# Four layer norms of a three-block kernel: two wide operations on VectorE in place of centring on ScalarE, gain on VectorE and bias on GpSimd

## What is computed

```python
def layer_norm(x, g, b):
    xf = x.astype(jnp.float32)
    mu = jnp.mean(xf, axis=-1, keepdims=True)
    var = jnp.mean(jnp.square(xf - mu), axis=-1, keepdims=True)
    return ((xf - mu) * lax.rsqrt(var + LN_EPS) * g + b).astype(x.dtype)
...
        # second block
        x = layernorm_2(DEEPNORM_ALPHA * x + mix, ln1_g[l], ln1_b[l])
        hid = jax.nn.silu(jnp.einsum('bsd,df->bsf', x, w_gate[l])) * jnp.einsum('bsd,df->bsf', x, w_up[l])
        ffn = jnp.einsum('bsf,fd->bsd', hid, w_down[l])
        x = layernorm_2(DEEPNORM_ALPHA * x + ffn, ln2_g[l], ln2_b[l])
...
        # third block
        x = layer_norm(DEEPNORM_ALPHA_3 * x + mix, ln1_g[l], ln1_b[l])
        xa = memory_cross_attention(x, mem, xa_wq[l], xa_wk[l], xa_wv[l], xa_wo[l])
        x = layer_norm(DEEPNORM_ALPHA_3 * x + xa, ln2_g[l], ln2_b[l])
        ff = hierarchical_moe(x, ...)
        x = layer_norm(DEEPNORM_ALPHA_3 * x + ff, ln3_g[l], ln3_b[l])
```

## Time and profile before

| | before |
|---|---|
| median of 3 runs | 3304.01 us (3303.87 to 3304.07) |
| the profiled execution | 3298.76 us |
| its span | 3297.1 us |
| TensorE busy | 3034.3 us, 92% |
| VectorE busy | 1455.9 us, 44% |
| ScalarE busy | 684.7 us, 21% |
| GpSimd busy | 131.8 us, 4% |
| mean granted TensorE clock | 0.953 |

### The profile page before, as it was taken

The page is one execution under the profiler, slowest core; times in us unless marked ns, Lnnn a source line. Parts: engine busy times, 40 slices in busy tenths (PEclk is TensorE's granted clock), DMA queues, the critical chain, the costliest instruction groups (busy, mean ns, idle before and its releaser), DMA issues. The chain is left out here.

```text
span 3297.1 us, 38666 instructions
## 1 busy us (share of the span) xinstructions
PE 3034.3 (92%) x15110; PEld 2168.6 (66%) x15110; DVE 1455.9 (44%) x2574; ACT 684.7 (21%) x1546; POOL 131.8 (4%) x148
## 2 busy tenths in 40 slices
PE   8779998999999889986999999998989986999997
PEld 4367765888868668885688887876766634333332
DVE  1564424324453667367543354424654232333335
ACT  1131112220010543570111001113531211111111
POOL 1000000000000200001000000000000011000000
PEclk9889999999999979997999999997889997999998
DMA  9112211223221102201223222222012107999995
GB/s 359 67 51 77 77 58 71 83 77 109 77 79 59 45 27 77 77 1 39 77 77 98 82 98 81 77 80 77 1 65 76 52 15 296 423 424 423 424 424 221
DMA packets 129894, 420.48 MB, mean 128 GB/s; under 512 B 6705, under 2 KB 35778, under 8 KB 108242
## 3 DMA queue, kind: packets, MB, share of 16 engines
q1 hardware_dynamic: 121842, 379.48, 30.1%
q10 hardware_dynamic: 3024, 23.59, 1.8%
q0 software_dynamic: 4880, 15.35, 1.3%
HBM read 394.81 MB, written 23.59 MB: 127 GB/s over the span
## 5 line engine op out<-in xcount | busy, mean ns | idle before, releaser
L775 PE MATMUL bank<-arena 128*128 128x256 f32 x5152 | 1125.3, 381 | 30.5 <-issue 15.5
L775 PEld LDWEIGHTS bank<-arena 128*128 128x128 f32 x5152 | 984.0, 191 | 172.1 <-issue 22.8
L1070 PE MATMUL bank<-arena 128*128 128x256 f32 x1652 | 358.7, 380 | 6.3 <-PEq L1217 2.7
L1070 PEld LDWEIGHTS bank<-arena 128*128 128x128 f32 x1652 | 314.6, 191 | 50.3 <-issue 7.4
L176 PE MATMUL bank<-arena 128*128 128x512 f32 (+7 forms) x804 | 252.1, 470 | 37.3 <-PEq L3297 11.5
L176 PEld LDWEIGHTS bank<-arena 128*128 128x128 f32 (+3 forms) x804 | 137.1, 195 | 146.7 <-issue 125.3
L423 PE MATMUL bank<-arena 128*128 128x512 f32 x384 | 167.7, 597 | 4.2 <-PEq L1622 2.0
L3737 DVE TENSOR_TENSOR arena<-arena,bank 128x512 f32<-128x512 f32 x128 | 87.7, 687 | 139.1 <-PE bank L3641 136.8
L839 DVE TENSOR_TENSOR arena<-arena 128x1024 f32<-128x1024 f32 x46 | 56.3, 1223 | 182.7 <-PE bank L775 179.3
L423 PEld LDWEIGHTS bank<-arena 128*128 128x128 f32 x384 | 73.1, 191 | 95.5 <-issue 95.5
L3641 PE MATMUL bank<-arena 128*128 128x512 f32 x256 | 123.2, 616 | 4.4 <-DVE arena L3723 4.4
(11 more groups left out here) (540 smaller groups left out, 3572.0 us busy)
## 6 DMA issues: line engine op xcount, KB each, us to landing
arena<-in_moe_w_gate_dram SPq DMA_DIRECT2D x64, 1024.0 KB, 16.4
arena<-in_moe_w_up_dram SPq DMA_DIRECT2D x64, 1024.0 KB, 18.5
arena<-in_moe_w_down_dram SPq DMA_DIRECT2D x32, 2048.0 KB, 23.9
arena<-in_w_in_dram SPq DMA_DIRECT2D x29, 2048.0 KB, 7.9
arena<-in_w_ff_dram SPq DMA_DIRECT2D x16, 2048.0 KB, 7.7
x_slots<-arena ACTq DMA_DIRECT2D x8, 2048.0 KB, 33.1
arena<-in_w_out_dram SPq DMA_DIRECT2D x8, 2048.0 KB, 7.7
arena<-in_w_gate_dram SPq DMA_DIRECT2D x11, 1024.0 KB, 5.4
```

What stands on the lines that cost most here:

```text
L775: last = pe.matmul(bank[:, m, :], lhsT, rhs, start=fresh and m == 0 and k == 0, stop=k == 3, skip_group_check=True)
L1070: last = pe.matmul(bank[:, m, :], x[:, k, m * P:(m + 1) * P], w[:, k, :], start=opening and m == 0 and k == 0, stop=k == w.shape[1] - 1, s ...
```

## The change

For every tile, VectorE now does `(x - mean) * gain` in one operation while ScalarE takes the root, then inverts the root, then does `x * inverse + bias` in a second one. ScalarE's centring, VectorE's shift and gain operations, GpSimd's bias additions and VectorE's extra bias addition for the last tile go, and with them their semaphores. VectorE's copy of tile i-2 now stands behind the tile's second wide operation, where it stood before the reciprocal. The diff of `down_and_layer_norm`; `sevens_and_layer_norm` is changed in the same way:

```diff
@@ down_and_layer_norm
         def ready(i):
-            return (normed, normed.at(i + 1)) if i < NT - 1 else (last_normed, last_normed.at(1))
+            return normed, normed.at(i + 1)
...
                 dve.tensor_scalar(sd[:, i:i + 1], mv[:, i, 1:2], 1.0, eps, ALU.mult, ALU.add).then_inc(var.sem,
                                                                                                        var.up())
+                if i == 0:
+                    dve.wait_ge(got.sem, got.at(32))
+                dve.scalar_tensor_tensor(out=x[:, i, :], in0=x[:, i, :], scalar=mv[:, i, 0:1], in1=gain, op0=ALU.subtract,
+                                         op1=ALU.mult).then_inc(gained.sem, gained.up())
+                dve.wait_ge(root.sem, root.at(i + 1))
+                dve.reciprocal(sd[:, i:i + 1], sd[:, i:i + 1]).then_inc(order.sem, order.up())
+                dve.wait_ge(order.sem, order.sent)
+                dve.wait_ge(gained.sem, gained.at(i + 1))
+                dve.scalar_tensor_tensor(out=x[:, i, :], in0=x[:, i, :], scalar=sd[:, i:i + 1], in1=bias, op0=ALU.mult,
+                                         op1=ALU.add).then_inc(normed.sem, normed.up())
                 if i >= 2:
                     empty_turned(dve, i - 2, 0).then_inc(emptied_v.sem, emptied_v.up())
-                dve.wait_ge(root.sem, root.at(i + 1))
-                dve.reciprocal(sd[:, i:i + 1], sd[:, i:i + 1]).then_inc(order.sem, order.up())
-                dve.wait_ge(order.sem, order.sent)
-                dve.scalar_tensor_tensor(out=shift[:, i:i + 1], in0=mv[:, i, 0:1], scalar=-1.0, in1=sd[:, i:i + 1],
-                                         op0=ALU.mult, op1=ALU.mult).then_inc(scaled.sem, scaled.up())
-                if i == 0:
-                    dve.wait_ge(got.sem, got.at(32))
-                dve.wait_ge(centred.sem, centred.at(i + 1))
-                dve.tensor_tensor(x[:, i, :], x[:, i, :], gain, ALU.mult).then_inc(gained.sem, gained.up())
-                if i == NT - 1:
-                    dve.wait_ge(gained.sem, gained.at(NT))
-                    dve.tensor_tensor(x[:, i, :], x[:, i, :], bias, ALU.add).then_inc(last_normed.sem, last_normed.up())
...
-            pool.wait_ge(got.sem, got.at(32))
-            for i in range(NT - 1):
-                pool.wait_ge(gained.sem, gained.at(i + 1))
-                pool.tensor_tensor(x[:, i, :], x[:, i, :], bias, ALU.add).then_inc(normed.sem, normed.up())
+        if meanwhile:
+            block.gpsimd(meanwhile)
...
                 act.activation(sd[:, i:i + 1], sd[:, i:i + 1], ACT.Sqrt).then_inc(root.sem, root.up())
-                act.wait_ge(scaled.sem, scaled.at(i + 1))
-                act.activation(x[:, i, :], x[:, i, :], ACT.Identity, bias=shift[:, i:i + 1],
-                               scale=sd[:, i:i + 1]).then_inc(centred.sem, centred.up())
```

More of the change, by code:

```diff
@@ L474, in down_and_layer_norm @@
     x, xT = c.x, c.xT
-    stats, mv, sd, shift = layer_norm_numbers(c)
+    stats, mv, sd, _ = layer_norm_numbers(c)
     gain, bias = rows[:, 0, :], rows[:, 1, :]
[L477 to L480, removed]
+    filled, got, var, root, gained, normed, turned, emptied = (c.sig(n) for n in (
+        "bank_filled", "rows_loaded_scalar", "variance_ready", "root_ready", "gain_applied", "normed", "rows_turned",
+        "bank_emptied_by_scalar"))
+    order, emptied_v = c.sig("vector_order"), c.sig("bank_emptied_by_vector")
     early = len(keys) - tail
@@ L1208, in sevens_and_layer_norm @@
     x, xT = c.x, c.xT
-    stats, mv, sd, shift = layer_norm_numbers(c)
+    stats, mv, sd, _ = layer_norm_numbers(c)
     gain, bias = rows[:, 0, :], rows[:, 1, :]
[L1211 to L1215, removed]
+    filled, got, var, root, gained, normed, turned, emptied = (c.sig(n) for n in (
+        "bank_filled", "rows_loaded_scalar", "variance_ready", "root_ready", "gain_applied", "normed", "rows_turned",
+        "bank_emptied_by_scalar"))
+    order, emptied_v, used = (c.sig(n) for n in ("vector_order", "bank_emptied_by_vector", "tile_added"))
     sevens = RowSevens(c, name, hidden, (1, 0), (5, 0), ((5, 3072), (5, 3584), (9, 2048), (9, 2560)), made)
@@ L1267, in _ @@
                                                                                                        var.up())
-                if i >= 2:
-                    empty_turned(dve, i - 2, 0).then_inc(emptied_v.sem, emptied_v.up())
+                if i == 0:
+                    dve.wait_ge(got.sem, got.at(32))
+                dve.scalar_tensor_tensor(out=x[:, i, :], in0=x[:, i, :], scalar=mv[:, i, 0:1], in1=gain, op0=ALU.subtract,
+                                         op1=ALU.mult).then_inc(gained.sem, gained.up())
                 dve.wait_ge(root.sem, root.at(i + 1))
@@ L1272, in _ @@
                 dve.wait_ge(order.sem, order.sent)
-                dve.scalar_tensor_tensor(out=shift[:, i:i + 1], in0=mv[:, i, 0:1], scalar=-1.0, in1=sd[:, i:i + 1],
-                                         op0=ALU.mult, op1=ALU.mult).then_inc(scaled.sem, scaled.up())
-                if i == 0:
-                    dve.wait_ge(got.sem, got.at(32))
-                dve.wait_ge(centred.sem, centred.at(i + 1))
-                dve.tensor_tensor(x[:, i, :], x[:, i, :], gain, ALU.mult).then_inc(gained.sem, gained.up())
-                if i == NT - 1:
-                    dve.wait_ge(gained.sem, gained.at(NT))
-                    dve.tensor_tensor(x[:, i, :], x[:, i, :], bias, ALU.add).then_inc(last_normed.sem, last_normed.up())
+                dve.wait_ge(gained.sem, gained.at(i + 1))
+                dve.scalar_tensor_tensor(out=x[:, i, :], in0=x[:, i, :], scalar=sd[:, i:i + 1], in1=bias, op0=ALU.mult,
+                                         op1=ALU.add).then_inc(normed.sem, normed.up())
+                if i >= 2:
+                    empty_turned(dve, i - 2, 0).then_inc(emptied_v.sem, emptied_v.up())
             for i in (NT - 2, NT - 1):
@@ L1284, in _ @@
             follow.dve(dve, ((emptied_v, NT), (emptied, NT)))
-        @block.gpsimd
-        def _(pool):
-            pool.wait_ge(got.sem, got.at(32))
-            for i in range(NT - 1):
-                pool.wait_ge(gained.sem, gained.at(i + 1))
-                pool.tensor_tensor(x[:, i, :], x[:, i, :], bias, ALU.add).then_inc(normed.sem, normed.up())
         @block.scalar
```

8 lines of the change are left out of this document (2 added, 6 removed).

## The result

The changed kernel takes 3311.84 us, the median of 14 runs (3300.39 to 3313.87); the kernel before, run beside it, took 3304.73 (14 runs, 3303.75 to 3306.56). The ratio is 1.0018, 95% interval [1.001, 1.0026]: slower by a small amount that can be told from nothing, and outside the forecast range of 3299.0 to 3307.5. The first profiled execution of the changed kernel took 3304.61 us (span 3302.8, clock 0.95), 7.2 us under its own median. That is the first thing to notice: this trace is not one of the usual executions.

The account below looks back on a forecast made before the run. PE was taken to bound the kernel, through its waits and its clock. Terms +2.25 (A), -0.56 (B), +0.30 (C), -2.7 (D) sum to -0.7 us; 3304.01 - 0.7 = 3303.3 us, range 3299.0 to 3307.5.

Parts of the forecast that it names:

- What bounds the kernel: TensorE (PE), busy 92% of the 3297.1 us span: time changes only where PE waits or where its clock does.
- What the change does to a tile: Each tile's norm takes 2.65 us from TENSOR_SCALAR to next operation; VectorE's copy, 0.68 us, becomes late at A, B and C.
- A: Second block's attention output layer norm: wait longer by 0.56 us, clock falls in sixteen matmuls (+1.69); +2.25 us in all.
- B: Second block's down projection layer norm: VectorE saves time per tile, PE starts earlier, gap shrinks to 4.28; -0.56 us.
- C: Layer norm of the third block's mixers' output: PE starts 0.55 us later at an already halved clock; +0.30 us taken.
- the third rival: At A to C PE goes by something earlier than VectorE's copy, so the change wins at all four places: 3300.3, chance 0.04.
- The second rival: Faster: the clock holds at A, 0.56 in place of 2.25, 3301.6; if also at D, 3298.8. Chance 0.20.
- D: Third block's cross attention layer norm, no follower: PE's turns start 2.08 us earlier and the clock recovers somewhat; -2.7 us.
- The constant of 5.25 us: Distance between the kernel before's profiled execution (3298.76 us) and the median of its runs (3304.01), treated as constant.
- The sum of -0.7 us: Total forecast change over the four layer norms: +2.25 - 0.56 + 0.30 - 2.7, with no further clock step.
- the first rival: Slower: PE's later start after A costs further clock steps between A and D, 1.69 each: 3305.0 or 3306.7; chance 0.30.
- The slower rival: The same as the first rival: one more clock step between A and D gives 3305.0, two 3306.7; chance 0.30.

Follow-up runs that it names:

- after_look_1: The changed kernel, without an edit, profiled again: median 3311.26 us over 8 runs, ratio 1.0016; its profiled execution took 3312.04 us.
- after_again: The changed kernel again, without an edit, beside the kernel before: 3312.07 us over 8 runs, ratio 1.0027; its profiled execution took 3300.49 us.
- one_more_copy_at_a: The kernel before, with ScalarE's copy of tile 1 at A made twice and nothing of the change: 3313.64 us, ratio 1.0033.

## Why the prediction was wrong, point by point

**What bounds the kernel: right.** Removing 20 us from ScalarE and 31 us from GpSimd moved nothing of its own. All that PE's shift shows is where PE waited and its clock.

**What the change does to a tile: right.** 2.65 us from TENSOR_SCALAR to the copy, wide operations of 1.27 to 1.29. VectorE's copy is last at A, B and C; the third rival fell.

**A: right, to 0.1 us.** Wait 4.25 (forecast 4.29), sixteen matmuls 5.41 (5.38), together +2.2 against +2.25. The price of the clock, taken from B, was the right one of the three named. The second rival, a clock that holds at A, did not happen in any of the four traces of the changed kernel.

**B: right** (-0.6 against -0.56). **C: right** (wait 5.33 against 5.35; the shift +0.1 and +0.4 against +0.30). **D: right in sum** (-2.8 and -3.0 against -2.7). The wait is 3.85, not 3.4, since PE gets through the turns of the tile before it 0.4 us earlier (before, these waited 0.22 us for GpSimd's bias), and the router's sixteen matmuls take 8.80 and 8.60 us in place of 9.54, so that the clock gave 0.7 to 0.9 back.

**The constant of 5.25 us: right for the kernel before.** It lies in the first 240 us. For the changed kernel the same subtraction would mislead: its three other profiled executions stand 0.8 above, 1.0 above and 11.6 below their medians, since an execution meets the step at 2357 us or doesn't; the one 11.6 below also had the low start, PE's shift -3.9 at 1600 us.

**The sum of -0.7 us is where it failed: terms that were put at nothing.** The step is the first rival, "one more such step costs what it cost at B, 1.69". That mechanism was named rightly: a PE that stands otherwise against the clock loses at further waits, in code that nothing touched; what failed is its price and that the forecast itself put it at nothing. One such step, at 1907 us, cost the +1.7 of that price; with it the sum is +1.0, and the first profiled execution of the changed kernel ends by its shift at +0.9 (from +0.3 to +1.2 in the table). The second, in the sparse attention, was mis-sized: 20.5 us of half clock instead of 3.4, +9.6 up to 2390 us, of which 2.3 come back up to 2435 us, where later low stretches are shorter: +7.3 in place of 1.69. The row that should have warned stands in the page: clock digits of 7, 8 and 8 in the three slices from 2226 to 2473 us, stretches of low clock far longer than behind B. The rival's own row warned too: 28 us at a mean of 0.63 are 28 x 0.37 = 10.4 us of missing clock, and it was priced at 1.69. I priced a step by the shortest one in the trace, where the longest ones set the upper end of the range. The sum of `after_look_1` is +0.7 at 1600 us, then +2.2 + 1.7 - 0.6 + 8.4 + 1.2 - 2.3 + 0.1 - 3.0 = +7.7, in all +8.4 by the steps listed and 8.5 by the shift; its time is 3312.04 - 3303.99 = 8.05 above.

**Rivals and chances.** The slower rival was the true one and had 0.30, the largest of the rivals; but its end was 3306.7. With the second step at its measured size it would have been about 3303.3 + 1.7 + 7.3 = 3312.3; that is hindsight, since no row of the trace before gives the 7.3. What the rows give is that a long step costs up to some 10 us, and a range with one such step would have held the time.

**What stays open.** Why the clock falls for 20.5 us behind a wait of 0.72 us in one execution and holds in another is not settled. By the place against the clock's last return the two differ by 0.02 us, and that sorts the traces at hand (above); the 0.33 us of shift, there from the first 240 us on, does not. The other execution without the step, after_again's, reached the wait 4.7 us before `after_look_1` did, so "later in the span loses" is no rule. The Trainium skill (the page named above, section "What's actually happening") says that the monitor is not restarted with the kernel, so that it matters where in its cycle work lands. The sorting of the traces by such a place agrees with that; no run here shows the cycle itself. I can't say why the kernel before met it in 11 runs of 29 at one time and in none of its 100 other runs (14, 30, 27, 21 and 8).

## What to carry to other kernels

- Where a change moves PE by a microsecond, list the stretches of low clock behind it, with the length of each, and let the missing clock of the longest bound the price of a step that may come or go. The local terms were right to 0.3 us here and the sum was off by 8.5.
- When work is taken from engines that don't bound, look for the copies that PE waits for and put them ahead of the new long operations. The same two operations a tile are worth +0.2% or -0.25%, by the place of a copy of 0.68 us.
- Compare traces only after looking at where their times stand among the runs. A profiled execution 7 us under its kernel's median doesn't contain the loss that is looked for.

## What was unexpected of the hardware

- A wait of 0.72 us, in 8.5 us in which PE was busy for 7.78, was followed by 20.5 us at 1.2 GHz; the same wait in another execution was followed by 0.99 of full clock. Against the clock's last return the two waits lie 0.02 us apart.
- 0.63 us of added wait at one place (A) cost 10.3 us by the median (`one_more_copy_at_a`), sixteen times its length.
- For the changed kernel a granted clock of 0.951 goes with 3299.4 to 3300.5 us, 0.950 with 3304.6, and 0.948 or 0.949 with 3310.3 to 3313.9, with nothing between 3304.6 and 3310.3.
- In the first 240 us two executions of the same code come to differ by 4.7 us, with a clock of 0.80 against 0.76 between 120 and 240 us.
